# A hybrid attention and mixture-of-experts block: output projection by contraction halves, expert weights in 2 MB transfers

## What is computed

```python
x = x + mixed @ w_out[l]                      # 256x1024 by 1024x1024
h2 = rmsnorm(x, norm2_w[l])
logits = (hf @ router_w) + router_b           # 32 experts
top_v, top_e = lax.top_k(logits, 4); top_w = softmax(top_v)
gu = xb @ w_gate_up[e] + b_gate_up[e]         # 1024x2048 for each expert
y  = ((up + 1.0) * glu) @ w_down[e] + b_down[e]   # 1024x1024 for each expert
return rmsnorm(x + moe, final_norm_w)
```

## Time and profile before

| | us |
|---|---|
| median of 3 runs | 1123.05 (1122.97 to 1123.39) |
| the profiled execution | 1123.45 |
| its span, first to last instruction | 1121.6 |
| TensorE busy | 1087.0 (97%) |
| VectorE, ScalarE, GpSimd busy | 348.6, 222.7, 47.8 |
| moved by the DMA engines | 438.92 MB, 391 GB/s over the span |
| chain that ended last | PE 68%, DMA 22%, DVE 2% |

### The profile page before, as it was taken

The page is one execution under the profiler, slowest core; times in us unless marked ns, Lnnn a source line. Parts: engine busy times, 40 slices in busy tenths (PEclk is TensorE's granted clock), DMA queues, the critical chain, the costliest instruction groups (busy, mean ns, idle before and its releaser), DMA issues.

```text
span 1121.6 us, 14718 instructions
## 1 busy us (share of the span) xinstructions
PE 1087.0 (97%) x6255; PEld 529.9 (47%) x6255; DVE 348.6 (31%) x686; ACT 222.7 (20%) x354; POOL 47.8 (4%) x38
## 2 busy tenths in 40 slices
PE   7999999999999999999999999999999998999997
PEld 7889888734343434344443424343333433343432
DVE  4894888522222130312222212120303022222212
ACT  6645775301010101010101010100010101011102
POOL 0392000000000000000000000000000000000000
PEclk9999999999999999999999999999999999999999
DMA  9547549799999999999999999999999999999996
GB/s 312 203 152 303 223 156 394 316 427 428 428 427 435 430 432 429 431 430 431 432 431 430 436 431 435 431 431 430 430 430 432 432 429 434 430 430 430 424 426 250
DMA packets 36066, 438.92 MB, mean 391 GB/s; under 512 B 2948, under 2 KB 5784, under 8 KB 20536
## 3 DMA queue, kind: packets, MB, share of 16 engines
q1 hardware_dynamic: 35104, 437.76, 92.7%
q10 hardware_dynamic: 920, 0.56, 0.2%
HBM read 437.25 MB, written 1.05 MB: 391 GB/s over the span
## 4 chain that ended last, share of the span: by engine, by line
PE 68%; DMA 22%; DVE 2%; issue 1%; ACT 0%; DVEq 0%; SPq 0%
PE PS L1790 31%; DMA W<-in_w_gate_up_dram 22%; PE PS L1851 14%; PE PS L1742 3%; PE PS L1762 3%; PE PS L1834 2%; PE PS L1449 2%; PE PS L1453 2%; PE PS L1456 2%; PE PS L1810 2%; PE PS L1435 1%; PE PS L1871 1%; DVE w_lo L460 0%; PE PS L1864 0%; PE PS L1702 0%
## 5 line engine op out<-in xcount | busy, mean ns | idle before, releaser
L1790 PE MATMUL PS<-W,M 128*64 128x512 f32 x2048 | 465.8, 607 | 19.2 <-DMA W<-in_w_gate_up_dram 13.7
L1790 PEld LDWEIGHTS PS<-W,M 128*64 128x64 f32 x2048 | 145.1, 139 | 309.7 <-issue 288.4
L1851 PE MATMUL PS<-W,M 128*64 128x512 f32 x1024 | 226.4, 594 | 1.1 <-DMA W<-in_w_down_dram 1.1
L1268 DVE TENSOR_SCALAR M<-PS 128x256 f32<-128x256 f32 x64 | 27.1, 423 | 523.5 <-PE PS L1790 523.5
L1851 PEld LDWEIGHTS PS<-W,M 128*64 128x64 f32 x1024 | 73.6, 137 | 138.7 <-issue 134.9
L852 ACT ACTIVATE M<-M 128x256 f32<-128x256 f32 x64 | 26.7, 417 | 484.9 <-DVE M L1268 484.9
L857 ACT COPY M<-PS 64x512 f32<-64x512 f32 x31 | 17.9, 578 | 260.4 <-PE PS L1851 260.4
L1284 DVE COPY M<-PS 128x512 f32<-128x512 f32 x32 | 22.1, 692 | 122.4 <-PE PS L1834 122.4
L1742 PE MATMUL PS<-M,X 128*128 128x128 f32 x480 | 57.6, 278 | 0.0
L1762 PE MATMUL PS<-M,SELT 128*128 128x512 f32 x120 | 55.8, 606 | 0.0
L1742 PEld LDWEIGHTS PS<-M,X 128*128 128x128 f32 x480 | 54.7, 192 | 1.0
(11 more groups left out here) (267 smaller groups left out, 849.9 us busy)
## 6 DMA issues: line engine op xcount, KB each, us to landing
W<-in_w_gate_up_dram SPq DMA_DIRECT2D x48, 4096.0 KB, 43.6
W<-in_w_down_dram SPq DMA_DIRECT2D x24, 4096.0 KB, 44.6
W<-in_w_gate_up_dram SPq DMA_DIRECT2D x32, 2048.0 KB, 14.9
W<-in_w_down_dram SPq DMA_DIRECT2D x14, 2048.0 KB, 14.3
raw<-in_w_in_dram SPq DMA_DIRECT2D x10, 2048.0 KB, 8.5
raw<-in_w_out_dram SPq DMA_DIRECT2D x2, 2048.0 KB, 10.4
W<-in_w_down_dram SPq DMA_DIRECT2D x3, 1024.0 KB, 43.4
raw<-in_w_in_dram SPq DMA_DIRECT2D x2, 1024.0 KB, 9.5
```

What stands on the lines that cost most here:

```text
L1268: v.tensor_scalar(gate[b], g2[:, :, 0], LIMIT, None, ALU.min).then_inc(gate_ready, 1)
L1790: ins = mm(gu[half][64 * g:64 * g + 64, :], hTe[:, k, tok], gu_slot[slot][:, kk, c:c + 512], start=(k == 0), stop=(k == KD - 1))
L1851: ins = mm(dst[64 * n:64 * n + 64, :], actT[b][:, 4 * kh + k, :], dn_slot[slot][:, k, 512 * n:512 * n + 512], start=(kh == 0 and k == 0), ...
```

## The change

**Output projection.** wo1 is split into two pieces of four row blocks and all 512 columns (place "KB") instead of two of 256 columns. `high1`, `rest1` and `low1` take a half `kh`. TensorE does the first half for both token tiles, then increments the new semaphore `half_used`, then the second half for both. The order behind is changed: turned x1T01 before the last low part, the four logits after wo11, x1T11 is copied out by ScalarE instead of VectorE, and VectorE's `chosen` is split in `highest` and the rest.

**Slots 6 and 10 of pair 0** are loaded as four transfers of 1 MB: their first halves after `half_used`, the second ones after wo11. TensorE waits for both.

**Pairs.** All units are loaded slot by slot, 2 MB each, and `arrived` waits for each slot. `add_residual` goes from pair 12 to pair 9 (`SUMMED`), and the branch from before pair 13 to before pair 10. Pairs 1 to 8 and 10 to 14 are loops, pairs 0, 9 and 15 written out.

```diff
+SUMMED = 9
-    ... [("wo1", j, "dve", ("B", j), None) for j in range(2)]
+    ... [("wo1", j, "dve", ("KB", j), None) for j in range(2)]
...
+            if buf == "KB":
+                return hi_b[:, 2048 * j:2048 * j + 2048].rearrange("p (k n) -> p k n", k=4)
...
-            return whole[:, :, 256 * j:256 * j + 256]
+            return whole[:, 4 * j:4 * j + 4, :] if what == "wo1" else whole[:, :, 256 * j:256 * j + 256]
...
-            filled(sp, "wo11")
-            for m in (6, 10):
-                load(0, 0, m)
+            for part in range(2):
+                if part:
+                    filled(sp, "wo11")
+                else:
+                    sp.wait_ge(half_used, 1)
+                c = slice(2048 * part, 2048 * part + 2048)
+                for m in (6, 10):
+                    sp.dma_start(slots(m)[:, c], slot_src(0, m)[:, c]).then_inc(slot_loaded[m] if part else half_loaded, 16)
             filled(sp, "lg1")
             sp.wait_ge(root2_ready, TT)
             load(0, 0, 9)
...
-            def load_pair(p, e, j, first_round, stop=12):
-                for m in range(0, stop, 2):
-                    if by_slots(j, m, first_round):
-                        for n in (m, m + 1):
-                            used(p + (n - SLOTS) // 12, (n - SLOTS) % 12)
-                            load(e, j, n)
-                    else:
-                        for n in (m, m + 1):
-                            used(p + (n - SLOTS) // 12, (n - SLOTS) % 12)
-                        load_unit(e, j, m)
+            def load_pair(p, e, j, stop=12):
+                for m in range(stop):
+                    used(p + (m - SLOTS) // 12, (m - SLOTS) % 12)
+                    load(e, j, m)
...
+            copy_out("x1T11", HT[:, 4:8, P:2 * P], bank("x1T11")[:].rearrange("p (k t) -> p k t", k=4))
...
             residual(0, 1)
-            turned_in(0)
+            turned_in()
+            residual(1, 1)
+            highest(0)
             chosen(0)
-            residual(1, 1)
-            turned_in(1)
+            highest(1)
             first_places(0)
             chosen(1)
             first_places(1)
...
-            ps = claim("wo01")
-            high1(ps, 0)
+            ps = [claim("wo01"), bank("wo11")]
+            high1(ps[0], 0, 0)
             turned_x1(0, 0)
-            rest1(ps, 0)
+            rest1(ps[0], 0, 0)
             turned_x1(1, 0)
-            low1(ps, 0)
-            ps = claim("wo11")
-            high1(ps, 1)
+            low1(ps[0], 0, 0)
+            claim("wo11")
+            high1(ps[1], 1, 0)
+            rest1(ps[1], 1, 0)
+            low1(ps[1], 1, 0).then_inc(half_used, 1)
+            high1(ps[0], 0, 1)
+            rest1(ps[0], 0, 1)
+            end(low1(ps[0], 0, 1), "wo01")
+            high1(ps[1], 1, 1)
+            rest1(ps[1], 1, 1)
             turned_x1(0, 1)
-            rest1(ps, 1)
+            end(low1(ps[1], 1, 1), "wo11")
             pe.wait_ge(router_ready, 1)
             logits(0, 0)
             logits(0, 1)
-            low1(ps, 1)
+            turned_x1(1, 1)
             logits(1, 0)
-            turned_x1(1, 1)
+            logits(1, 1)
+            keep_clock(bank("wo11"), 384)
             places(0)
...
-                if m % 2 == 0:
-                    pe.wait_ge(slot_loaded[m], 16 * (j + 1) if isinstance(r, int) else r * (16 * PAIRS) + 16 * (j + 1))
-                elif not isinstance(j, int):
-                    return slot
...
+                if isinstance(r, int) and isinstance(j, int) and j == 0 and m in (6, 10):
+                    pe.wait_ge(half_loaded, 32)
+                pe.wait_ge(slot_loaded[m], 16 * (j + 1) if isinstance(r, int) else r * (16 * PAIRS) + 16 * (j + 1))
...
-                for j in range(PAIRS - 3, PAIRS - 1):
+                with pe.Fori(SUMMED + 1, PAIRS - 1) as j:
                     pair(0, j)
                 pair(0, PAIRS - 1, last=True, final=True, only=only)
...
-            for j in range(3):
-                pair(0, j)
-            with pe.Fori(3, PAIRS - 4) as j:
-                pair(0, j)
-            pair(0, PAIRS - 4, residual=True)
+            pair(0, 0)
+            with pe.Fori(1, SUMMED) as j:
+                pair(0, j)
+            pair(0, SUMMED, residual=True)
```

More of the change, by code:

```diff
@@ L55 @@
     [("mu", j, "dve", ("QA", j), "gb1") for j in range(4)] + [("hu", j, "dve", ("QD", j), "gb3") for j in range(4)] + \
-    [("wo0", j, "dve", ("A", j), "mu3") for j in range(2)] + [("wo1", j, "dve", ("B", j), None) for j in range(2)]
+    [("wo0", j, "dve", ("A", j), "mu3") for j in range(2)] + [("wo1", j, "dve", ("KB", j), None) for j in range(2)]
 AT_PIECE = {(p[0], p[1]): n for n, p in enumerate(PIECES)}
@@ L86, in bank_units @@
     u += [("wo00", "dve"), ("wo10", "dve"), ("x1T00", "act"), ("x1T10", "act"), ("wo01", "dve"), ("x1T01", "dve"),
-          ("lg0", "dve"), ("wo11", "dve"), ("x1T11", "dve"), ("pos0", "dve"), ("lg1", "dve"), ("pos1", "dve"),
+          ("wo11", "dve"), ("lg0", "dve"), ("x1T11", "act"), ("lg1", "dve"), ("pos0", "dve"), ("pos1", "dve"),
           ("all", "dve"), ("wT", "dve")]
@@ L435, in ring @@
             return m
[L439 to L445, removed]
         def unit_src(e, m):
@@ L532, in used @@
                     sp.wait_ge(weights_used, p * 8 + (m - m // 4 if m < 8 else 6 + (m - 8) // 2) + 1)
-            def load_pair(p, e, j, first_round, stop=12):
-                for m in range(0, stop, 2):
-                    if by_slots(j, m, first_round):
-                        for n in (m, m + 1):
-                            used(p + (n - SLOTS) // 12, (n - SLOTS) % 12)
-                            load(e, j, n)
-                    else:
-                        for n in (m, m + 1):
-                            used(p + (n - SLOTS) // 12, (n - SLOTS) % 12)
-                        load_unit(e, j, m)
+            def load_pair(p, e, j, stop=12):
+                for m in range(stop):
+                    used(p + (m - SLOTS) // 12, (m - SLOTS) % 12)
+                    load(e, j, m)
             last = PAIRS - 1
             for j in range(1, last):
-                load_pair(j, 2 * j, j, True)
-            load_pair(last, E - 2, last, True, stop=10)
+                load_pair(j, 2 * j, j)
+            load_pair(last, E - 2, last, stop=10)
             parts = [(10, 0, 2, slot_loaded[10]), (10, 2, 4, part_loaded[0]),
@@ L567, in _ @@
                         for j in range(1, PAIRS):
-                            load_pair(r * PAIRS + j, 2 * j, j, False)
+                            load_pair(r * PAIRS + j, 2 * j, j)
             sp.wait_ge(x_free, 1)
@@ L1168, in residual, with turned_in, highest @@
                 drain(name, v.tensor_tensor(xs, bank(name)[:].rearrange("p (q k) -> p q k", k=4), xs, ALU.add))
[L1170 to L1176, removed]
+            def turned_in():
+                filled(ve, "x1T01")
+                drain("x1T01", v.tensor_copy(HT[:, 4:8, 0:P], bank("x1T01")[:].rearrange("p (k t) -> p k t", k=4)))
+            def highest(tt):
                 ve.wait_ge(root2_ready, tt + 1)
@@ L1187, in chosen @@
                 st.settle()
+            def chosen(tt):
+                lt, g, q = lg[:, tt, :], gt[:, tt, :], eq[:, tt, :]
                 v4 = top8[:, tt, TOPK - 1:TOPK].to_broadcast([P, E])
@@ L1647, in keep_clock, with high1, rest1, low1 @@
                 mm(free_bank[:, 0:cols], ident, rows_of(0)[:, 0:cols], start=True, stop=True)
[L1649 to L1668, removed]
+            w1_h = hi_b.rearrange("p (k n) -> p k n", k=KD)
+            w1_l = w_lo[LOADS.index("wo1") % RING].rearrange("p (k n) -> p k n", k=KD)
+            def high1(ps, tt, kh):
+                pe.wait_ge(hi_ready, AT_PIECE["wo1", kh] + 1)
+                for k in range(4 * kh, 4 * kh + 4):
+                    mm(ps[:], mix_hi[:, k, P * tt:P * tt + P], w1_h[:, k], start=(k == 0), stop=False)
+            def rest1(ps, tt, kh):
+                wait_lo("wo1", kh)
+                for k in range(4 * kh, 4 * kh + 4):
+                    mm(ps[:], mix_hi[:, k, P * tt:P * tt + P], w1_l[:, k], start=False, stop=False)
+            def low1(ps, tt, kh):
+                for k in range(4 * kh, 4 * kh + 4):
+                    ins = mm(ps[:], mix_lo[kh][:, k - 4 * kh, P * tt:P * tt + P], w1_h[:, k], start=False, stop=(k == KD - 1))
+                return ins
             def turned_x1(tt, half):
@@ L1725, in _ @@
             keep_clock(bank("wo11"), 384)
-            logits(1, 1)
             pe.wait_ge(first_sel_ready, 1)
             first_gather(0, 0)
+            places(1)
             first_gather(0, 1)
-            places(1)
-            keep_clock(bank("wo11"), 384)
             pe.wait_ge(sel_ready, 1)
```

9 lines of the change are left out of this document (1 added, 8 removed).

## The result

The changed kernel takes 1125.06 us (median of 20 runs, 1123.94 to 1127.67) against 1123.24 for the kernel before in the same comparison (20 runs, 1122.39 to 1123.85): a ratio of 1.0017, 95% interval 1.0011 to 1.0023. That is 1.8 us slower; 1.7 had been forecast. The profiled execution took 1124.0 us with a span of 1122.2, at the low end of its runs, so the span alone (0.6 us more than before) understates the difference.

What follows compares the result with a forecast made beforehand. The prediction took the DMA engines to bound the kernel from end to end. Its terms, -2.7 + 5.7 + 0.2 + 0 - 1.5 = +1.7 us on 1123.05, gave 1124.8 us, range 1121.0 to 1128.9.

Steps and rivals of the forecast that it cites:

- What bounds: Whole kernel: DMA engines bound it from end to end; TensorE savings in between are worth nothing.
- (1): Output projection: half loads fill the DMA hole at 210 us; 2.7 us gained, bounds 0 and 3.4, landing margin 3.7 us.
- new hole in pair 0: Sign of being wrong: the DMA queue running dry in pair 0, instead of its share staying full at 225 and 274 us.
- Rival A: Pair 0: the hole moves on if it starts 1 us or more after 220.6; 1128.9 us, chance 0.13.
- (2): Weight loads: 72 units of 4 MB as 144 transfers of 2 MB; 5.7 us more, bounds 4.9 and 6.6.
- (3): Pairs: a TensorE wait for each slot, six more per pair, shifts stops but costs nothing at the end.
- (4): Residual sums to pair 9, branch after it, pairs looped: hidden at either place; bounds 0 and -0.5 us.
- (5): Pairs as loops: some 16 instruction fetches for 21, one less on the slowest engine; 1.5 us gained, bounds 0 and 3.
- B: Closing sums: TensorE let down to half clock, some 4 us more, 1128.5 us; chance 0.07.
- C: Cheap end: full front gain, transfer price 4.9 us, three fetches' worth and half a microsecond; 1121.3 us, chance 0.16.
- D: Weight loads: transfer size costs nothing, the two rates differ by their stretches; 1119.1 us, chance 0.03.
- E: Weight loads: 2 us for each of 72 further transfers, 144 us in all; 1263 us, chance 0.01.

Runs made afterwards that it cites:

- e7: Changed kernel with the residual sums back in pair 12 and the branch before pair 13; 1124.90 us, ratio 1.0017 to the kernel before.
- e10: Changed kernel with TensorE waiting for both slots of a unit at once in pairs 1 to 14, transfers still 2 MB; 1125.12 us.
- e2: Kernel before with every 4 MB unit as two 2 MB transfers, each with its own wait; 1128.82 us, ratio 1.0049.
- e9: Kernel before with each unit still one 4 MB transfer, but read in 16 KB runs instead of 32 KB; 1128.83 us, ratio 1.0053.
- e8: Kernel e1 with less code, residual sums between two loops and pair 15's units at 4 MB too; 1123.54 us, ratio 1.0006 to the kernel before.
- e12: Kernel before with the changed front alone; 4 MB units, loops and residual sums as before; 1120.79 us, ratio 0.9984.
- e3: Changed kernel with slots 6 and 10 of pair 0 loaded whole after wo11, no half loads; 1125.40 us, ratio 1.0022 to the kernel before.
- e4: Changed kernel with pairs 1, 2, 13 and 14 written out instead of looped; 1126.21 us, ratio 1.0027 to the kernel before.
- e11: Kernel e8 with pair 15 loaded slot by slot again; 1119.05 us, ratio 0.9969 to the kernel before.
- e1: Changed kernel with 4 MB units and single waits again in pairs 3 to 14, pairs 1 and 2 written out; 1120.65 us, ratio 0.9982 to the kernel before.
- e5: Kernel before with each 4 MB unit as two 2 MB transfers of 64 partitions each, 32 KB rows; 1860.68 us, ratio 1.654.

## Why the prediction was right

Sign and size were right (+1.7 forecast, +1.8 measured), and the terms can be checked one by one. The transfers' term is right with its mechanism; that of the front is right in size by two errors that nearly cancel, which is luck.

*What bounds.* Right. e7 and e10 change TensorE's schedule by up to 10.8 us and the time by less than 0.3; e2 and e9 change the DMA rate by 0.7% and the time by 5.6 us. But "from end to end" is too much. e8 marks one end, the last pair, where TensorE's own work sets the end once it starts late; the other is pair 0, where TensorE's releases decide whether the queue runs dry.

*(1) The front.* -2.7 + 0.2 forecast, -2.4 measured (e12). The reason given was only half right. I counted 3.4 us won in the hole by the half loads and 0.7 given back. The stretches show 3.3 us won in the hole (66 to 420 GB/s) and 1.1 us ahead of it (376 to 421), which the forecast did not have, and 1.5 us given back (0.3, 0.6 and 0.6 from 213.5 to 223.5, 223.5 to 240 and 270 to 280 us), twice what it had. From 190 to 280 us the changed kernel has moved 1.10 MB more, 2.6 us at 428 GB/s. What was given back is the new hole in pair 0 that the forecast named as a sign of being wrong: it stands there, at 398 and 397 GB/s, and the DMA share there is 0.97 and 0.98, not full. And a part of the gain is not the half loads' at all but comes from the router's matmuls moved behind wo11 (e3), which the forecast used in its time for wo11, 209.7, and did not name. The landing of the slot issued near 273 us shows the thin stock. It was 10.9 us in the earlier trace rows and is now

```profile
W<-in_w_down_dram SPq DMA_DIRECT2D x1, 2048.0 KB, 8.7
```

of which 7.2 are the price into an empty queue. The margin was priced for the slowest engine, and the text said it was less for the others; that was the right worry. Rival A took it to be the whole of (1), and for the median it was wrong: pair 0 begins at 219.86 us in the profiled execution, and e12 gains 2.4 us. Single executions come near it. In the profiled execution of e10 pair 0 began at 222.62, past A's mark, and it took 1127.98 us, where A had 1128.9.

*(2) The transfers.* +5.7 forecast, read off one row of 90 us and one of 300; +5.64 measured (e2). What I left open, whether packets or transfers cost, e9 settles for packets. The slow issues came into the middle as forecast: the chain of the changed kernel has one of 4.24 us before its long DMA piece,

```profile
663.53 4.24 SPq L468
...
667.81 49.53 DMA W<-in_w_gate_up_dram
```

and the queue behind it is full all the same. The Trainium skill's fixed 2.0 us for a DMA (DMA: Bandwidth & Descriptors, Anatomy of one DMA), which the section fits for transfers issued by GpSimd and not, as all of these, by SyncE, would have made e2 144 us slower: 0.078 us was measured for a further transfer with a queue behind it.

*(3) and (4).* Zero forecast, 0.1 and 0.2 us measured (e10, e7).

*(5) The code.* -1.5 forecast, called the softest term. Three readings bear on it: 1.15 us by e4; 1123.2 + 5.6 - 2.4 = 1126.4 without it against 1125.1 measured, so 1.3 us for (4) and (5) together; and e11 against e1, 1.6 us with two bodies less. They agree on 1 to 1.6 us, but each is a difference of medians whose intervals are about 1 us wide to either side. The count of packets was off, 13 for the 16 forecast; the forecast's own two and a half a pair for five bodies would have given 13. So eight fetches less, and not five, go with this gain. That single engines are held up is an inference from the longer fall-off of the DMA share, not shown engine by engine.

Of the rivals, B did not come about. TensorE's waits for weights from 600 us on in the changed kernel (us in total, times, longest), and its stretch from 600 to 900 us, where the clock was 0.97 before:

```profile
PE PS L1782 <- DMA W<-in_w_gate_up_dram: 12.3, 17, 1.2
PE PS L1843 <- DMA W<-in_w_down_dram: 11.1, 11, 1.3
...
600.00:900.00 300.00, 288.14 (x1580) 113.23 (x1577) 60.84 (x155) 28.62 (x51) 0.00 (x0) 1.00 1.01 428
```

No stop is longer than 1.34 us and the clock is full; the half clock after a stop of 2.55 us is gone with that stop. It brings nothing, since it was covered. The row of 1112 to 1116 us above shows the closing sums at a clock of 1.00 as well. C's 1121.3 lies below all 20 runs of the changed kernel (the lowest is 1123.94); its low price of 4.9 alone is not excluded, since e2's interval is 4.0 to 7.1 us. D and E are excluded by e2.

## What to carry to other kernels

When the DMA queue never empties, price a change by bytes and packets, not by waits: here each further packet cost an engine 9 to 10 ns, and 10 us of TensorE's work in the middle cost nothing. TensorE counts where it releases the first slots and in the last pair. A hole in such a queue is worth its length only if the queue's later stock does not live on it; look at the shortest time from issue to landing behind the hole and compare it with a lone transfer's. Use large runs in the middle and fine grain only in the last stage, where a wait for two slots at once puts the other engine's work behind the last landing.

## What the runs showed of the hardware that was not expected

- A transfer over 64 of the 128 partitions moved 211 GB/s with the DMA engines busy all the time, against 431 over 128 partitions with the same 32 KB rows (e5). Two such halves in the queue one after the other do not make up for each other.
- The price of a packet is steady: 432, 428 and 421 GB/s with runs of 32, 16 and 8 KB, whether the 16 KB runs come in one transfer of 4 MB or two of 2 MB.
- Kernels with the new front spread more from run to run: 3.7 us in the changed kernel, 2.7 in e1, 3.2 in e12 against 1.5 in the kernel before and 0.4 in e2 (from 20, 11 and 11 runs against 20 and 5). e3 spreads by 2.7 too, so the half loads are not the reason. The ten profiled executions with this front point to TensorE's clock just ahead of pair 0. In seven of them it is 1.00 from 209.5 to 223.5 us, pair 0 begins between 219.8 and 220.3 us, and the time is at or below the kernel's median. In three (e4, e7, e10) it falls to 0.50 near 213 us for 3 to 7 us, pair 0 begins at 220.7, 220.8 and 222.6, the stretch from 223.5 to 240 us moves 370, 367 and 321 GB/s (398 in the changed kernel), and the time is 0.8, 0.8 and 2.9 us above the median. TensorE was busy without a stop from 209 us on in these three, so what brings the clock down is not seen, and nothing was tried. e10's stretches, then the start of pair 0 in e10 and in the changed kernel:

```profile
213.50:223.50 10.00, 10.00 (x51) 8.04 (x52) 4.76 (x23) 1.10 (x4) 0.00 (x0) 0.67 1.01 423
223.50:240.00 16.50, 15.26 (x74) 5.26 (x70) 5.15 (x21) 1.70 (x2) 0.00 (x0) 1.00 0.80 321
...
222.62 3.58 PE PS L1783 x15
...
219.86 10.45 PE PS L1782 x48
```
